# Joining the even and the odd mixer's input stage with the stage that follows in a two-stack Trainium2 kernel

## What is computed

```python
def second_block(x, mem, ...):
    for layer in range(2):
        hn = rms_norm(h, norm_mix[layer])
        h = h + (even_mixer(hn) if layer == 0 else odd_mixer(hn))
        h = h + mem_cross_attention(rms_norm(h), rms_norm(mem), ...)
        h = h + peer_ffn(rms_norm(h), ...)        # 8 heads x 16 experts per token, rows gathered
    return rms_norm(h, norm_final)

def even_mixer(hn, ...):
    z, xbc, dt_raw, xm, og, ig, fg = split(hn @ w_in)   # 1024, 1536, 16, 1024, 1024, 4, 4 columns
    y_a = ssd_mixer(z, xbc, dt_raw, ...)    # conv of 4 taps, silu, state space in 2 chunks, 16 heads
    y_b = mlstm_mixer(xm, og, ig, fg, ...)
    return concatenate([y_a, y_b]) @ w_out

def hgrn2_mixer(uq, uf, ui, ug, lb, norm_w):            # 8 heads of 128, 4 chunks of L = 64
    logf = log(lb + (1 - lb) * sigmoid(uf)); k = (1 - lb) * sigmoid(-uf); q = silu(uq); v = ui
    gc = cumsum(logf, within the chunk); g_ref = gc[middle]
    att = causal((q * exp(gc - g_ref)) @ (k * exp(g_ref - gc)).T)
    s_local = (k * exp(gc[last] - gc)).T @ v            # state: s = exp(gc[last]) * s + s_local
    o = att @ v + (q * exp(gc)) @ s_prev
    return head_rms_norm(o, norm_w) * silu(ug)
```

## Time and profile before

| | |
|---|---|
| median of 3 runs | 3499.24 us (3492.52 to 3500.0) |
| the profiled run's own time, and its span | 3499.23 us, 3497.5 us |
| TensorE, weight loads | 2772.5 us (79%), 2006.5 us (57%) |
| VectorE | 2261.9 us (65%) |
| ScalarE | 970.2 us (28%) |
| GpSimd | 622.6 us (18%) |
| mean granted TensorE clock | 0.897 |
| moved from memory | 807.44 MB |

### The profile page before, as it was taken

The page is one execution under the profiler, slowest core; times in us unless marked ns, Lnnn a source line. Parts: engine busy times, 40 slices in busy tenths (PEclk is TensorE's granted clock), DMA queues, the critical chain, the costliest instruction groups (busy, mean ns, idle before and its releaser), DMA issues. The chain is left out here.

```text
span 3497.5 us, 36438 instructions
## 1 busy us (share of the span) xinstructions
PE 2772.5 (79%) x13624; PEld 2006.5 (57%) x13624; DVE 2261.9 (65%) x4109; ACT 970.2 (28%) x1528; POOL 622.6 (18%) x547
## 2 busy tenths in 40 slices
PE   8988999987899898798676766667669866666665
PEld 7857987966897787587442222226458743222222
DVE  5375545547554553654778888865544578888886
ACT  4353434426343462343211000003424310000000
POOL 0000000000000000000244444440000034444442
PEclk9989999998999898899888888898779988888888
DMA  6512454440454440153589999994314289999996
GB/s 233 175 49 100 167 179 152 172 153 2 149 188 148 149 169 13 54 176 115 221 330 421 421 421 421 421 421 159 132 45 161 73 310 385 421 420 421 421 421 287
DMA packets 112353, 810.86 MB, mean 232 GB/s; under 512 B 12720, under 2 KB 12720, under 8 KB 14000
## 3 DMA queue, kind: packets, MB, share of 16 engines
q0 software_dynamic: 73728, 536.90, 37.3%
q1 hardware_dynamic: 38448, 271.63, 21.8%
HBM read 807.44 MB, written 1.05 MB: 231 GB/s over the span
## 5 line engine op out<-in xcount | busy, mean ns | idle before, releaser
L160 DVE TENSOR_TENSOR ring_low<-ring,parts 128x2048 fp32r<-128x2048 f32 x234 | 533.6, 2291 | 433.0 <-ACT parts L153 430.7
L415 PE MATMUL ps<-parts,parts 128*128 128x256 f32 x2944 | 657.1, 284 | 8.0 <-DVE ring_low L160 8.0
L2706 PE MATMUL ps<-arena 128*128 128x512 f32 x768 | 448.9, 741 | 234.2 <-DVE arena L2599 234.2
L2706 PE MATMUL ps<-ring,arena 128*128 128x512 f32 x768 | 433.2, 716 | 215.9 <-DVE arena L2599 215.9
L415 PE MATMUL ps<-parts,ring_low 128*128 128x256 f32 x2080 | 584.5, 281 | 0.0
L153 ACT ACTIVATE parts<-ring 128x2048 fp32r<-128x2048 f32 x234 | 444.2, 1912 | 365.6 <-PE ps L423 159.3
L423 PE MATMUL ps<-parts,parts 128*128 128x512 f32 x1536 | 499.9, 400 | 40.0 <-DVE ring_low L160 18.9
L415 PEld LDWEIGHTS ps<-parts,parts 128*128 128x128 f32 x2944 | 497.2, 190 | 10.0 <-issue 10.0
L2706 PEld LDWEIGHTS ps<-arena 128*128 128x128 f32 x768 | 174.2, 237 | 506.7 <-DVE arena L2599 314.5
L2706 PEld LDWEIGHTS ps<-ring,arena 128*128 128x128 f32 x768 | 164.4, 225 | 479.6 <-DVE arena L2599 305.9
L415 PEld LDWEIGHTS ps<-parts,ring_low 128*128 128x128 f32 x2080 | 394.8, 190 | 0.0
(11 more groups left out here) (403 smaller groups left out, 2870.1 us busy)
## 6 DMA issues: line engine op xcount, KB each, us to landing
ring<-in_stream SPq DMA_DIRECT2D x249, 1024.0 KB, 4.8
arena<-in_experts,stage_index POOLq DMA_INDIRECT x256, 24.5
ring<-in_experts,stage_index POOLq DMA_INDIRECT x256, 25.1
gain_row<-in_gain_rows SPq DMA_DIRECT2D x4, 512.0 KB, 5.0
arena<-in_mem SPq DMA_DIRECT2D x2, 1024.0 KB, 6.6
arena<-in_stream SPq DMA_DIRECT2D x2, 1024.0 KB, 7.0
par<-in_params SPq DMA_DIRECT2D x4, 386.0 KB, 3.1
x<-in_x SPq DMA_DIRECT2D x1, 1024.0 KB, 5.1
```

Of the source, the lines that this page charges most:

```text
L160: dve.tensor_tensor(k.ring_low[v % SLOTS], whole, self.high[:, c % self.HIGH_SLOTS, :].bitcast(F32), ALU.subtract).then_inc(self.ph.sem("c ...
L415: last = pe.matmul(self.ps[:, 2 * pair + f // 2, (f % 2) * T:(f % 2 + 1) * T], w[:, f * P:(f + 1) * P], x[:, k, :], start=(k == 0 and i == ...
L2706: last = pe.matmul(k.ps[:, bank + n, :], diag[:, s % ROWS, :], rows[row_of[s]][:, D + n * BLK:D + (n + 1) * BLK], start=(s % SLOTS_PER_TOK ...
```

## The change

It does four things. The two phases of the even layer become `even_mixer_phase`: the weights come in the order xbc, xm, z, og; the matmuls of the state space stand between the linear groups; the work on the decay goes by halves (8 heads of a chunk); `keep_busy` with its 104 matmuls is gone, and with it one barrier. The two phases of the odd layer become `odd_mixer_phase`: the reciprocal on VectorE is replaced by Ln(1 + e) and Exp(-) on ScalarE; the exponentials, transposes, scores and own parts stand between the linear groups; there are three slots for states, so that the three local products come without a wait between; ScalarE copies the own part; the norm goes by halves. In `peer`, SyncE in layer 0 waits until the gathers of the last group, two, have landed before it loads the ring. A few tiles get other places. ScalarE's program has 81 loads of function tables where it had 75. Cut to its core:

```diff
-STREAM_2 = ([("ssd_z", 8, 2), ("xbc", 8, 3), ("xm", 8, 2), ("og", 8, 2), ("ml_wq", 4, 1), ("ml_wk", 4, 1),
+STREAM_2 = ([("xbc", 8, 3), ("xm", 8, 2), ("ssd_z", 8, 2), ("og", 8, 2), ("ml_wq", 4, 1), ("ml_wk", 4, 1),
...
+                k.linear_group(pe, ph, lx, parts, True, None, split, 0, norm)
...
+                k.linear_group(pe, ph, lx, parts, True, None, split, 1)
+                pe.wait_ge(ph.sem("small_copied"), 1)
+                pe.wait_ge(ph.sem("dta_ready"), 1)
...
+                rows(0)
+                k.linear_group(pe, ph, lx, parts, True, None, split, 2)
+                rows(1)
+                k.linear_group(pe, ph, lm, parts, True, None, split, 0)
+                pe.wait_ge(ph.sem("x_active"), 3)
...
+                last.then_inc(ph.sem("cb_done"), 1)
+                pe.wait_ge(ph.sem("rows_taken"), 2)
+                k.transposes(pe, ph, "x", jobs, [6, 7])
+                k.linear_group(pe, ph, lm, parts, True, None, split, 1)
+                pe.wait_ge(ph.sem("sums_taken"), 1)
+                pe.wait_ge(ph.sem("x_scaled"), 1)
+                own(0)
+                pe.wait_ge(ph.sem("x_copied"), 5)
+                rows(2)
+                k.linear_group(pe, ph, lz, parts, False, None, split, 0)
+                own(1)
+                rows(3)
+                k.linear_group(pe, ph, lz, parts, False, None, split, 1)
+                pe.wait_ge(ph.sem("rows_taken"), 4)
+                pe.wait_ge(ph.sem("late_ready"), 1)
...
+                last.then_inc(ph.sem("states_done"), 1)
+                own(2)
+                k.linear_group(pe, ph, lo, parts, False, None, split, 0)
+                own(3)
+                pe.wait_ge(ph.sem("states_ready"), 1)
...
+                last.then_inc(ph.sem("carried_done"), 1)
+                k.linear_group(pe, ph, lo, parts, False, None, split, 1)
...
+                taps(1)
+                silu(0)
+                taps(2)
+                silu(1)
+                act.wait_ge(ph.sem("sums_taken"), 1)
...
+                decays(0)
+                decays(1)
+                silu(2)
+                taps(3)
+                for i in range(4):
...
+                taps(4)
                 for n in range(2):
...
+                    split.high_for(act, lz, n)
...
+                    silu(3 + n)
+                    decays(2 + n)
+                split.high_for(act, lo, 0)
+                squares(0)
...
+                squares(1)
+                k.rstd_scalar(act, ph, link, ms, y)
...
+                mask(0)
+                convolve(1)
+                split.low_for(dve, lx, 2)
+                mask(1)
+                convolve(2)
+                split.low_for(dve, lm, 0)
+                mix(0)
+                mix(1)
+                dve.wait_ge(ph.sem("x_copied"), 4)
...
+                link(dve.tensor_tensor(z.xs, z.xs, bc(z.dt.unsqueeze(3), [P, MT, 16, HD]), ALU.mult))
+                dve.sem_inc(ph.sem("x_scaled"), 1)
+                split.low_for(dve, lm, 1)
                 dve.wait_ge(ph.sem("ends_exp"), 1)
...
+                dve.tensor_tensor(late, z.xs[:, 0], bc(z.dend.unsqueeze(2), [P, 16, HD]), ALU.mult).then_inc(ph.sem("late_ready"), 1)
+                convolve(3)
+                take_own(0)
+                mask(2)
+                convolve(4)
+                split.low_for(dve, lz, 0)
+                take_own(1)
+                mask(3)
+                split.low_for(dve, lz, 1)
+                mix(2)
+                dve.wait_ge(ph.sem("states_done"), 1)
...
+                mix(3)
+                take_own(2)
+                dve.wait_ge(ph.sem("z_ready"), 2)
+                link(dve.tensor_tensor(z.ya[:, 0, :], z.ya[:, 0, :], z.z[:, 0, :], ALU.mult))
                 dve.sem_inc(ph.sem("y_ready"), 1)
...
+                split.low_for(dve, lo, 1)
+                take_own(3)
+                dve.wait_ge(ph.sem("carried_done"), 1)
...
-                    k.keep_busy(pe, 4, 16)
...
-                        k.keep_busy(pe, 4, 20)
...
-                k.linear_tok(pe, ph, lg, parts, split=split)
+                pe.wait_ge(ph.sem("keys_decayed"), 1)
+                k.transposes(pe, ph, "kd", jobs, [4, 5])
+                pe.wait_ge(ph.sem("operands_ready"), 1)
+                att(0)
+                k.linear_group(pe, ph, lg, parts, False, None, split, 0)
+                pe.wait_ge(ph.sem("v_copied"), 2)
+                pe.wait_ge(ph.sem("kd_copied"), 4)
+                own(0)
+                att(1)
+                k.linear_group(pe, ph, lg, parts, False, None, split, 1)
+                pe.wait_ge(ph.sem("own_taken"), 1)
+                own(1)
...
+                for c in range(3):
...
+                    if c > 0:
+                        pe.wait_ge(ph.sem("gate_ready"), c)
...
+                    last.then_inc(ph.sem("local_done"), 1)
+                pe.wait_ge(ph.sem("own_taken"), 2)
+                for c in range(1, 4):
+                    pe.wait_ge(ph.sem("state_ready"), c)
...
+                    last.then_inc(ph.sem("carried_done"), 1)
...
-                act.wait_ge(ph.sem("f_sigmoid"), 1)
+                act.wait_ge(ph.sem("f_bounded"), 1)
+                link(act.activation(z.e2, e, ACT.Ln, bias=1.0))
+                link(act.activation(z.e2, z.e2, ACT.Exp, scale=-1.0))
+                act.sem_inc(ph.sem("f_sigmoid"), 1)
...
+                act.sem_inc(ph.sem("q_silu"), 1)
+                act.wait_ge(ph.sem("to_end"), 1)
+                act.activation(z.e1, z.e1, ACT.Exp).then_inc(ph.sem("to_end_exp"), 1)
+                split.high_for(act, lv, 0)
+                act.wait_ge(ph.sem("to_middle"), 1)
...
+                link(act.activation(qg, z.e2, ACT.Exp))
+                link(act.activation(z.e2, z.fT, ACT.Exp, scale=-1.0))
+                link(act.activation(z.fT, z.fT, ACT.Exp))
+                act.sem_inc(ph.sem("middle_exp"), 1)
...
-                link(dve.reciprocal(z.fT, z.fT))
...
+                split.low_for(dve, lv, 0, ahead=0)
...
                 link(dve.tensor_tensor(e1, end, gc, ALU.subtract))
                 dve.sem_inc(ph.sem("to_end"), 1)
+                link(dve.tensor_tensor(middle, gc, ref, ALU.subtract))
+                dve.sem_inc(ph.sem("to_middle"), 1)
                 dve.wait_ge(ph.sem("to_end_exp"), 1)
                 link(dve.tensor_tensor(e1, e1, kT, ALU.mult))
                 dve.sem_inc(ph.sem("keys_decayed"), 1)
...
+                split.low_for(dve, lv, 1, ahead=0)
                 dve.wait_ge(ph.sem("middle_exp"), 1)
+                dve.wait_ge(ph.sem("q_silu"), 1)
...
                 link(dve.tensor_tensor(qg, qg, z.qT, ALU.mult))
...
+                link(dve.tensor_tensor(z.qT, z.qT, z.fT, ALU.mult))
+                dve.sem_inc(ph.sem("queries_ready"), 1)
+                link(dve.tensor_tensor(z.kT, z.kT, z.e2, ALU.mult))
                 dve.sem_inc(ph.sem("operands_ready"), 1)
...
+                split.low_for(dve, lg, 0, ahead=0)
+                mask(0)
+                split.low_for(dve, lg, 1, ahead=0)
+                mask(1)
+                state(1)
+                state(2)
+                dve.wait_ge(ph.sem("own_taken"), 2)
+                carry(1)
                 dve.sem_inc(ph.sem("y_ready"), 1)
+                state(3)
+                dve.wait_ge(ph.sem("gate_ready"), 2)
+                carry(2)
                 dve.wait_ge(ph.sem("squares_summed"), 1)
...
+                k.rstd_vector_before(dve, ph, link, ss[:, 0], ms[:, 0], P)
+                carry(3)
+                dve.sem_inc(ph.sem("y_ready"), 1)
+                link(dve.tensor_tensor(gated, z.y, z.gate, ALU.mult))
+                finish(0)
+                dve.wait_ge(ph.sem("squares_summed"), 2)
+                k.rstd_vector_before(dve, ph, link, ss[:, 1], ms[:, 1], P)
+                finish(1)
...
+                if first + SLOTS < CHUNKS_2:
+                    for s in range((GROUPS - 1) * PER_GROUP, GROUPS * PER_GROUP):
+                        row = row_of[s]
+                        sp.wait_ge(k.gathered[row], 16 * (layer + 1) * row_of.count(row))
```

604 lines of the change are left out of this document (266 added, 338 removed).

## The result

| | before | changed |
|---|---|---|
| median | 3499.03 us (3492.52 to 3500.0, 4 runs) | 3382.36 us (3379.89 to 3383.72, 4 runs) |
| profiled run, its span | 3499.23, 3497.5 | 3383.28, 3381.5 |
| mean granted clock | 0.897 | 0.908 |

What follows compares the result with a forecast made beforehand. TensorE paces the input stages; in the state-space and recurrence stages engines wait in turn. Savings of 30.6 (even), 47.4 (odd) and 10.0 (gathers), 88.0 in all, from 3499.23 give 3411 us; range 3399 to 3438 for 8 in 10.

Steps and rivals of the forecast that it cites:

- Bound now: TensorE paces the input stages, with groups 11.16 or 11.32 apart; in the state-space and recurrence stages engines wait in turn.
- Even, "32.2 stay": Joined even stage: of the state-space stage's 55.08 on TensorE, 22.9 of filler falls away and 32.2 stays, without waits.
- Even, the stall of 5.8: Even stage, third transpose: TensorE waits 5.8 for a bank that ScalarE's copy frees behind high parts, a copy and taps.
- Odd, the walk: Joined odd stage, followed queue by queue from the second f group to the last product: 162.6 before, 47.4 saved.
- the 3.4 for slow local products: Odd stage: charge for two local products at 3.78 rather than 2.05.
- Gathers: Layer 0's last four rows: ring loads moved behind the gathers save 10.0, and the loads stay hidden.
- rival 2: Ring loads start 15 later and run into the odd stage's need, giving back the 10: 3421, chance 0.08.
- The unknown, the clock: TensorE's clock between groups: no fall gives 3402; one fall of 2.6 at some ten places costs 26, not 8.
- 1 (a fall at every thin stretch): TensorE's clock falls at each stretch of thin work between groups, 18 more: 3429, chance 0.20.
- 5 (low clock throughout): Joined stages run at the lower clock throughout, 17 groups cost 161 more, net +73: 3572, chance 0.02.
- 3: Each ScalarE table switch also drains it, seven on the way at 1.28 more, 9 in all: 3420, chance 0.04.
- 4: VectorE's hand-made order puts a convolution of some 5 ahead of needed work three times, 15: 3426, chance 0.04.

Runs made afterwards that it cites:

- The doubling: Even layer's rows of sums, own parts, states and carried part issued twice, in the changed kernel (3401.55 us) and in the kernel before (3523.32 us).
- The odd layer's doubling: Recurrence's scores, own parts, locals and carried parts issued twice, in the kernel before (3512.40 us) and in the changed kernel (3396.41 us).
- The whole again: The changed kernel, unaltered, timed again beside the kernel before: 3379.41 us against 3497.59, ratio 0.966.
- the parts: Kernel before with only the even layer joined (3454.64 us), only the odd layer joined (3438.43), or only SyncE's gather wait added (3487.55).
- the copies of x first: Changed kernel with ScalarE's copies of turned x before the fourth group's taps, and small exponentials and first decay work behind them: 3385.62 us, ratio 0.9685.

## Why the prediction was wrong

The direction, the places and the mechanism were right, and the size was outside the range. Step by step:

- **Bound now.** TensorE's pace of 11.16 and 11.32 for a group held in the joined stages, with 3.5 of other matmuls before each of the last four groups of the even layer.
- **Even, "32.2 stay".** This term failed. Taking from 134.0 the groups (89.9), the small matmuls (9.4), the slow group behind them (2.5), the tail (2.3) and the waits (5.4 and 0.9) leaves 23.6 for the moved matmuls and the clock around them, where I charged 32.2 and 3. The rows of sums, own parts, states and carried part by themselves were busy for 27.7 in the separate stage (9.5, 10.9, 3.7, 3.6) and for 19.4 in the joined one (8.0, 7.6, 1.9, 1.9). I had taken the busy time of a stage whose clock was 0.83 as the price of its work. I read that clock in the very row and then used it only as a reason for charges on top, though it was one for a discount. The doubling shows it: 16.6 against 25.8. I also left the own parts, 64 columns wide, out of the widths I named, and they have the largest part in it.
- **Even, the stall of 5.8.** Right in place and size: 5.4, and 0.9 for a Silu ahead of it.
- **Odd, the walk.** In us behind the second f group's end:

| | forecast | measured |
|---|---|---|
| logarithms end | 19.3 | 19.4 |
| scan ends | 23.8 | 23.9 |
| TensorE's wait at v | 3.4 | 4.3 |
| first g group ends | 65.7 | 66.6 |
| second g group ends | 80.9 | 81.3 |
| last local product ends | 89.1 | 87.8 |
| last carried part ends | 100.0 | 96.3 |
| stage ends, without charges | 108.9 | 105.1 |
| stage ends, with charges | 115.3 | 105.1 |

  Up to the last group the walk is within 0.9, in part because two errors cancel: TensorE didn't wait 1.2 at v's second low part, but behind the wait of 4.3 the clock did fall, to 0.57 over 4 us, and the two v groups took some 1.6 longer than at their usual pace. Behind the last group two terms fail. The own part and three local products, four times 2.05 in the sum, took 6.5 in one run; the carried parts, which I priced at 3.55 from a row that begins behind a wait, took 3.33 for two in one run and 2.86 for the third. And of the charges, the 3.4 for slow local products didn't come, and the 3 for the waits would only have been the 1.6 above, since the clock is at 1.0 from there to the last carried part:

```profile
2397.60:2401.60 4.00, 3.57 (x9) 2.89 (x10) 4.00 (x3) 1.69 (x2) 0.00 (x0) 0.57 0.67 283
2401.60:2452.00 50.40, 49.23 (x246) 40.97 (x245) 30.62 (x16) 26.20 (x20) 0.00 (x0) 1.00 0.41 146
2452.00:2465.40 13.40, 11.01 (x103) 10.39 (x102) 6.95 (x19) 5.98 (x20) 0.00 (x0) 1.00 0.24 79
```

  The odd layer's doubling doesn't prove this, these rows of the changed kernel do.
- **Gathers.** 9.9 for 10.0, and the loads stayed hidden (rival 2 falls). My rate for them, 2.6 apiece, was a misreading: each of the eight had waited for its own slot in these 21.09, and once all slots are free they are issued within 4.07.
- **The unknown, the clock.** The bound "no fall at all" was 3402 because it only gave back the charges. The true lower bound would have priced the moved matmuls at 2.4 GHz throughout, from the kernel before: its second rows of sums, at 1.00, took 3.84 for 32 where the first took 5.65, and its state matmuls, at 0.50, halve from 3.7 to the 1.9 that they took later. A linear group's matmuls of the same 512 columns are no measure for these (11.16 for 48, so 0.23 apiece; a state matmul took 0.47 at 1.00).
- **Rivals.** 1 (a fall at every thin stretch) and 5 (low clock throughout) fall: windows at 1.0 beside the own and state parts. The Trainium skill, "TensorE: Matmul & The Clock Gate", section "HAM oscillation — how this bites in real kernels", says that gaps between bursts bring the clock down; I had cited it and not put it in the sum. The windows agree with it, 0.63 behind waits in the kernel before against 1.0 between groups in the changed one; the small matmuls, which lose the clock without a gap (last section), don't fit it. 3 falls too: in the even stage the operation ahead of the load ends at 1205.08, the load begins at 1205.10, takes 1.28, and its operation follows at 1206.39, so the drain that the Trainium skill, "ScalarE: Activation LUTs", section "What ACT_TABLE_LOAD costs", adds doesn't show here either. 4: no convolution held up a low part for more than the group hid.
- **What is left.** Some 7 of the 116.7 lie outside the three places. The profiled run of before was at the upper end: over the 16 traces of the kernels behind it the first stack, which none of them changes, is from 6.8 shorter to 1.1 longer than in it. The whole again measured 118.2, though, and the parts sum to 106.9; whether the 7 are chance or something the change does to the rest stays open within these intervals.

## What to carry to other kernels

The busy time of a stage that waits a lot isn't the price of its work: TensorE's matmuls there run in part at 1.2 GHz. When such work is moved between full groups, price it from rows at clock 1.0 (or halve those at 0.5), and let the range begin there. A walk through the queues, engine by engine, gave the two large waits within a microsecond (5.4 for 5.8, 4.3 for 3.4) and one of 1.2 that never came. The local product put ahead of a full group lengthened by 2.2 what stood before the group's end, so it pays only where it shortens the rest by more. And a difference of 2 us between two stages was no more than chance here until both had the clock fall at the same matmuls.

## What the runs showed of the hardware

TensorE can lose its clock while it is busy without a gap: in the changed kernel the small matmuls, 24 columns wide, begin at 1.00 and end at 0.50, and TensorE is busy throughout.

```profile
1195.50:1198.30 2.80, 2.80 (x27) 2.80 (x27) 0.00 (x0) 2.68 (x5) 0.00 (x0) 1.00 0.63 193
1201.70:1205.00 3.30, 3.30 (x16) 3.30 (x17) 0.00 (x0) 0.13 (x1) 0.00 (x0) 0.50 0.02 5
```

And it can stay low while it is busy: in the doubled separate stage 64 own matmuls of 64 columns in a row, behind a wait of 2.52, ran at 0.50 for 13.8 us, though 64 of the rows of sums, 128 columns wide and behind a wait of 1.37, ran at 1.0 in the same stage:

```profile
1344.40:1351.70 7.30, 7.30 (x65) 7.30 (x66) 2.43 (x2) 0.00 (x0) 0.00 (x0) 1.00 0.01 2
1361.70:1375.50 13.80, 13.80 (x65) 13.80 (x66) 0.00 (x0) 0.00 (x0) 0.00 (x0) 0.50 0.01 1
```

In the joined stage with the doubling the same own matmuls stand in pieces of 32 with groups around them and no wait ahead, and kept 1.0 (14.7 for 128 of them). A short piece by itself isn't enough: with the copies of x first, 16 own matmuls behind a wait of 5.2 took 3.64, for 1.89 without a wait. So narrow matmuls want to stand close behind full groups; how much of this is the missing wait and how much the neighbours, no run here separates.
